# Hybrid decoder trunk: five split chunks and seven loaded ones, and the fourth block ahead of the down chunk

## What is computed

```python
for i in range(4):                     # stick-breaking, differential, forgetting, stick-breaking
    x = x + 0.5 * swiglu(rms_norm(x, norm_g[i, 0]), gate[i, 0], up[i, 0], down[i, 0])
    q, k, v = split(rms_norm(x, norm_g[i, 1]) @ w_qkv[i])
    x = x + attention_i(q, k, v) @ w_o[i]
    x = x + 0.5 * swiglu(rms_norm(x, norm_g[i, 2]), gate[i, 1], up[i, 1], down[i, 1])
return rms_norm(x, final_g)
# x: 256 tokens x 1024, d_ff 2816, 8 heads of 128, float32; swiglu(h) = (silu(h@gate) * (h@up)) @ down
```

## Time and profile before

| | |
|---|---|
| time, 3 runs | median 1882.12 us (1881.24 to 1883.84) |
| profiled execution, its own time | 1877.97 us |
| its span, first to last instruction | 1876.2 us |
| busy in the span | PE 1853.3, weight loads 1566.1, DVE 1562.6, ACT 1166.9, POOL 60.3 us |
| granted TensorE clock | 0.999 of full speed |
| DMA | 417 MB, mean 222 GB/s |

### The profile page before, as it was taken

How to read it: one execution, slowest core, us unless ns; L and a number is a source line. 1 busy time by engine, 2 the same in 40 slices (tenths; PEclk the granted TensorE clock), 3 DMA queues, 4 the chain that set the end, 5 groups by cost and what they waited for, 6 DMA issues and landing times.

```text
span 1876.2 us, 22732 instructions
## 1 busy us (share of the span) xinstructions
PE 1853.3 (99%) x9268; PEld 1566.1 (83%) x9268; DVE 1562.6 (83%) x1295; ACT 1166.9 (62%) x1220; POOL 60.3 (3%) x75
## 2 busy tenths in 40 slices
PE   9999999999999999999999999999999999999998
PEld 7788898888878899788888888987888888998886
DVE  7979568989888969998988995788898898569896
ACT  6666456666656645666665674465667567556665
POOL 1000000000000000100000000010000000001000
PEclk9999999999999999999999999999999999999999
DMA  8775445776677543577667763467775766437762
GB/s 300 261 290 226 180 157 180 226 289 264 200 249 272 235 151 134 183 254 286 266 187 272 255 247 121 149 227 245 270 278 190 274 221 246 157 108 252 277 238 79
DMA packets 59272, 417.28 MB, mean 222 GB/s; under 512 B 7192, under 2 KB 7456, under 8 KB 8992
## 3 DMA queue, kind: packets, MB, share of 16 engines
q1 hardware_dynamic: 53968, 380.09, 51.8%
q0 software_dynamic: 4608, 33.56, 9.5%
q10 hardware_dynamic: 592, 2.17, 0.3%
HBM read 414.74 MB, written 1.06 MB: 222 GB/s over the span
## 4 chain that ended last, share of the span: by engine, by line
PE 80%; DVE 12%; DMA 4%; ACT 2%; issue 2%; POOL 0%; SPq 0%; POOLq 0%; DVEq 0%; ACTq 0%
PE work L1493 16%; PE work L1495 16%; PE work L1494 16%; PE acc L1493 9%; PE acc L1495 9%; PE acc L1494 9%; DVE w_lo L919 6%; DMA extra<-stream_dram 3%; DMA raw<-stream_dram 1%; PE work L1687 1%; DVE raw L935 1%; PE acc L1537 1%; DVE raw L931 1%; PE work L1865 1%; PE work L1729 0%
## 5 line engine op out<-in xcount | busy, mean ns | idle before, releaser
L919 DVE TENSOR_TENSOR w_lo<-raw,w_hi 128x2048 fp32r<-128x2048 f32 x359 | 810.3, 2284 | 14.2 <-ACT w_hi L535 14.0
L535 ACT ACTIVATE w_hi<-raw 128x2048 fp32r<-128x2048 f32 x359 | 677.1, 1910 | 128.7 <-DVE raw L935 76.2
L1493 PE MATMUL work<-w_hi,xg 128*128 128x512 f32 x880 | 346.6, 394 | 1.1 <-DVE w_lo L919 1.1
L1495 PE MATMUL work<-w_hi,xg 128*128 128x512 f32 x880 | 343.5, 390 | 0.0
L1494 PE MATMUL work<-w_lo,xg 128*128 128x512 f32 x880 | 343.0, 390 | 0.0
L1493 PE MATMUL acc<-w_hi,m_hi 128*128 128x512 f32 x824 | 328.3, 398 | 6.3 <-DVE w_lo L919 6.1
L1495 PE MATMUL acc<-w_hi,m_lo 128*128 128x512 f32 x824 | 321.8, 391 | 0.0
L1494 PE MATMUL acc<-w_lo,m_hi 128*128 128x512 f32 x824 | 321.2, 390 | 0.0
L1495 PE MATMUL work<-w_hi,wide_r 128*128 128x512 f32 x512 | 199.8, 390 | 0.0
L1493 PEld LDWEIGHTS work<-w_hi,xg 128*128 128x128 f32 x880 | 165.4, 188 | 34.9 <-DVE w_lo L919 1.7
L1495 PEld LDWEIGHTS work<-w_hi,xg 128*128 128x128 f32 x880 | 165.3, 188 | 34.8
(11 more groups left out here) (211 smaller groups left out, 2324.8 us busy)
## 6 DMA issues: line engine op xcount, KB each, us to landing
raw<-stream_dram SPq DMA_DIRECT2D x295, 1024.0 KB, 7.3
extra<-stream_dram SPq DMA_DIRECT2D x64, 1024.0 KB, 4.9
extra<-stream_dram POOLq DMA_DIRECT2D x32, 1024.0 KB, 8.0
x<-x_dram SPq DMA_DIRECT2D x2, 512.0 KB, 8.2
raw<-stream_dram ACTq DMA_DIRECT2D x2, 512.0 KB, 8.0
scratch<-cum_rows ACTq DMA_DIRECT2D x1, 1024.0 KB, 6.5
cst<-consts_dram SPq DMA_DIRECT2D x1, 832.0 KB, 6.4
out_dram<-x SPq DMA_DIRECT2D x3, 256.0 KB, 2.5
```

What stands on the lines that cost most here:

```text
L535: nc.scalar.activation(w_hi[:, c % RING, :], raw_at(place), ACT.Copy).then_inc(hi_ready, 1)
L919: nc.vector.tensor_tensor(w_lo[:, c % RING, :], raw_at(place), w_hi[:, c % RING, :].bitcast(F32), ALU.subtract).then_inc(lo_ready, 1)
L1493: nc.tensor.matmul(dst, a_hi, b_hi, start=start, stop=False, skip_group_check=skip)
L1495: return nc.tensor.matmul(dst, a_lo, b_hi, start=False, stop=stop, skip_group_check=skip)
```

## The change

The ring of split chunks has five places, not six, and there are seven buffers of loaded chunks, not five. In the first pair of a chain b22 stands ahead of the down chunk, on PE and in the ring. With it, ACT and DVE treat the block c12 ahead of c21 in such a pair, and DVE makes the form t3' after `gate_21`. The load of b22' is listed ahead of b21' (before: after the down chunk). Where unit 1 is followed by the chain, DVE makes t3 and the third low part of the token sums before `hidden_lo(0)` in all FFNs but the first. In the differential attention a chunk is split earlier, on ACT before `mix`, on DVE before `apart_mean` and the early updates. At the end of the run the squares and the scaled output are taken from the accumulators, without the halved copy.

```diff
-RAW = 5
+RAW = 7
-RING = 6
+RING = 5
@@ pair_order, first pair of a chain
-    return [..., ("t3", s), ("down", s - 1), ("t4", s), ("b22", s)]
+    return [..., ("t3", s), ("b22", s), ("down", s - 1), ("t4", s)]
@@ plan
+            if what == "t4" and j in SEVEN[:-1] and not chained(following(j)):
+                loads.append(("b22", layer, n % 3, following(j), EXTRA, ("lo", c0 + order.index(("b22", j)) + 1)))
+            if what == "b21" and chained(j):
+                loads.append(("b22", layer, n % 3, j, EXTRA, ("lo", c0 + order.index(("b22", j - 2)) + 1)))
             for load in ("b12",) if what == "t1" else () if what in (*FORMS, "b22") else (what,):
...
-            if what == "down" and chained(j + 2):
-                loads.append(("b22", layer, n % 3, j + 2, EXTRA, ...))
...
-            if what == "t4" and j in SEVEN[:-1] and not chained(following(j)):
-                loads.append(("b22", layer, n % 3, following(j), EXTRA, ...))
@@ ACT, pair_step, first pair
                     silu_22()
+                    split_to(q + 9)
+                    silu_12()
                     split_to(q + 10)
                     silu_21()
                     split_to(q + 11)
-                    silu_12()
@@ ACT, last norm
-                        update(n, i)
-                        square_sum(n, i)
+                        last_square_sum(i)
@@ DVE, plain_step(1), not in the first FFN
+                        token_sums_lo((0, 1, 2))
                     form("t3", q)
+                        hidden_lo(0)
@@ DVE, first_of_chain
                         if s == SEVEN[0]:
                             hidden_lo(s - 1)
-                        split_to(q + 5)
-                        if s == SEVEN[0]:
                             token_sums_lo((3,))
                         split_to(q + 6)
                         gate_11()
                         sum_22()
                         split_to(q + 7)
+                        sum_12()
                         split_to(q + 8)
                         gate_22()
-                        split_to(q + 9)
+                        gate_12()
+                        split_to(q + 10)
+                        gate_21()
                         form("t3", q + 8)
-                        gate_21()
-                        sum_12()
-                        split_to(q + 10)
                         form("t2", q + 8)
-                        gate_12()
                         hidden_lo(s)
                         split_to(q + 11)
@@ DVE, end of the differential attention
                         apart_split(b)
+                        split_to(c0 + ATT_CHUNKS + 1)
+                        apart_mean()
                         for i in range(BANKS - 1):
                             early_update(i)
-                        apart_mean()
-                        split_to(c0 + ATT_CHUNKS + 1)
@@ PE, pair_step, first pair
                     quarter(chain, sum_of(S3), at["t3"], False, False)
+                    if s == SEVEN[0]:
+                        pe.wait_ge(token_lo_ready, BANKS * (f + 1))
+                    quarter(3, sum_of(S4), at["b22"], False, True)
                     unit_down(s - 1).then_inc(down_used, 1)
                     pe.wait_ge(pair_sums_ready, 2 * p + sum_count("c22"))
                     quarter(chain, block_of(1, 1), at["t4"], False, True)
-                    if s == SEVEN[0]:
-                        pe.wait_ge(token_lo_ready, BANKS * (f + 1))
-                    quarter(3, sum_of(S4), at["b22"], False, True)
```

More of the change, by code:

```diff
@@ L76, in pair_order @@
                 ("down", s - 1), ("t4", s)]
-    return [("b11", s), ("t1", s), ("t2", s), ("b21", s), ("t3", s), ("down", s - 1), ("t4", s), ("b22", s)]
+    return [("b11", s), ("t1", s), ("t2", s), ("b21", s), ("t3", s), ("b22", s), ("down", s - 1), ("t4", s)]
 def following(s):
@@ L85, in part_count, with block_count @@
     return [part for part, unit in pair_order(s) if unit == s].index(what) + 1
-def block_count(s, which):
-    return (("c11", "c22", "c12", "c21") if chained(s) else ("c11", "c22", "c21", "c12")).index(which) + 1
+def block_count(which):
+    return ("c11", "c22", "c12", "c21").index(which) + 1
 def sum_count(which):
@@ L184, in plan @@
                 loads.append((load, layer + 1, 0, SEVEN[0], place, ("lo", c0 + order.index((last, SEVEN[-1])) + 1)))
-            if what == "down" and chained(j + 2):
-                loads.append(("b22", layer, n % 3, j + 2, EXTRA, ("lo", c0 + order.index(("b22", j)) + 1)))
             if what == "down" and j + 1 in SEVEN[:-1]:
                 loads.append(("b11", layer, n % 3, following(j + 1), SUMS, ("lo", c0 + order.index(("t1", j + 1)) + 1)))
-            if what == "t4" and j in SEVEN[:-1] and not chained(following(j)):
-                loads.append(("b22", layer, n % 3, following(j), EXTRA, ("lo", c0 + order.index(("b22", j)) + 1)))
     return uses, loads
@@ L795, in attention @@
                         weights(b)
+                    if j == PAIRS and kind == DIFF:
+                        split_to(c0 + ATT_CHUNKS + 1)
                     if j < PAIRS:
@@ L830, in square_sum, with last_square_sum @@
                 nc.scalar.activation(squares[i % 2], x_part(bank), ACT.Square, scale=D ** -0.5,
+                                     accum_out=sums[:, bank // TB, bank % TB:bank % TB + 1]).then_inc(squares_ready, 1)
+            def last_square_sum(i):
+                n, bank = NORMS - 1, banks_of(NORMS - 1)[i]
+                act.wait_ge(acc_ready, BANKS * (n - 1) + i + 1)
+                act.wait_ge(squares_ready, BANKS * n + i - 1)
+                nc.scalar.activation(squares[i % 2], acc[:, bank, :], ACT.Square, scale=D ** -0.5,
                                      accum_out=sums[:, bank // TB, bank % TB:bank % TB + 1]).then_inc(squares_ready, 1)
@@ L1038, in plain_step @@
                     q = c0 + FFN_ORDER.index(("b11", s + 1))
-                    if s == 1:
+                    if s == 1 and n:
+                        token_sums_lo((0, 1, 2))
+                    elif s == 1:
                         token_sums_lo((0, 1))
@@ L1455, in next_input @@
                     final_output(0, 0)
+                    final_mean(1)
                     final_gained()
-                    final_mean(1)
                     final_output(0, 1)
@@ L1463, in final_mean @@
                 dve.wait_ge(squares_ready, BANKS * (NORMS - 1) + 2 * tb + 2)
-                nc.vector.scalar_tensor_tensor(out=mean[:, tb:tb + 1], in0=sums[:, 0, tb:tb + 1], scalar=EPS,
+                nc.vector.scalar_tensor_tensor(out=mean[:, tb:tb + 1], in0=sums[:, 0, tb:tb + 1], scalar=4 * EPS,
                                                in1=sums[:, 1, tb:tb + 1], op0=ALU.add,
@@ L1471, in final_output @@
                 dve.wait_ge(final_loaded, 16)
-                part = x_part(TB * half + tb)
-                nc.vector.scalar_tensor_tensor(out=part, in0=part, scalar=r_col[:, tb:tb + 1],
+                bank = TB * half + tb
+                nc.vector.scalar_tensor_tensor(out=x_part(bank), in0=acc[:, bank, :], scalar=r_col[:, tb:tb + 1],
                                                in1=final_gain[:, half * HALF_D:(half + 1) * HALF_D],
@@ L1682, in pair_hidden @@
                     for block in ("c12", "c22") if second else ("c11", "c21"):
-                        pe.wait_ge(pair_h_ready, 4 * p + block_count(first, block))
+                        pe.wait_ge(pair_h_ready, 4 * p + block_count(block))
                     for t in range(2):
```

21 lines of the change are left out of this document (11 added, 10 removed).

## The result

The changed kernel took 1867.06 us in the median of 5 runs (1866.86 to 1867.81), the kernel before 1881.24 us in 5 runs (1874.98 to 1883.84). The ratio is 0.9926 with a 95% interval of 0.9911 to 0.9942: faster by 14.2 us. The profiled execution of the changed kernel took 1867.57 us, 10.4 us less than that of before (1877.97). Note also the spread: 8.9 us before, 0.95 us after. In the changed kernel the lines have other numbers: the matmuls L1493 to L1495 are L1504 to L1506, the split L919 is L929, t3's form L931 is L941, `gate_21` L1084 is L1098.

A forecast was written before the change was run, and what follows sets the result against it. PE, busy 99% of the span, bounds the kernel, so only its waits can be won. Chains 6.8, first FFN 1.7 and end 0.6 sum to 9.1 us off 1882.1: 1873.0 us, range 1868 to 1881.

The forecast's parts named there:

- The chain's source: At unit 2 of later FFNs: DVE idles 3.33 us for b22' before t3', and later work queues behind it.
- The chains, 6.8 us: Chains after the first FFN: 5.0 us of listed PE waits times 1.36, all won; bounds 5.0 and 7.5.
- The load "which SP could issue only at 525.02": Load of b22', third FFN: issued once b22 was split; issue moves from 17.25 to 10.9 after b11, taking 8.0 us.
- "The median of the runs is 4.15 us above that execution, so 1882.1 - 9.1": Whole run: the 9.1 us gain is taken off the median of 1882.1 us, giving 1873.0.
- Differential attention, "nothing gained or lost": DVE's earlier split before `apart_mean` ends at 761.25, before PE's sums at 761.6, so no gain or loss.
- First FFN, 1.7 us: First FFN: gain of 1.7 us out of 5.3 us of listed PE waits; bounds 0 and 5.3.
- Tail 0.6: End of the run: ACT's 0.60 us halving leaves the path after the last matmul, gaining 0.6 us.
- Seams 0: Ends of FFNs under the ring of five: no cost taken; bounds 0 and 0.6 us for each of seven seams.
- Rival A: Ring short of room: ACT's copies wait for places, chains lose 0.85 us each; 1879 to 1883 us, chance 0.09.
- Rival B: POOL's accumulating DMA lands late, beyond 12.5 us, delaying t1' and DVE; at 14.5 us 1891, slower, chance 0.11.
- Rivals C and D: C: chains still lose 0.1 to 0.2 us, 1874.6 to 1877.9, chance 0.12. D: load still waits, 1881.5, chance 0.04.
- The sign of being wrong: PE's waits behind `w_lo` staying above 4 us would show the forecast to be wrong.

The follow-up runs named there:

- Experiment 4: The kernel before, unaltered, measured again with two more profiled executions: 1880.56 us in 12 runs, the profiled ones 1883.98 and 1876.51 us.
- experiment 2: The kernel before with only the two sizes changed, ring of five and seven buffers of loaded chunks: 1870.53 us, 0.9947 of before.
- experiment 3: The kernel before with the ring of five and six buffers of loaded chunks: 1872.61 us, 0.9961 of before.
- experiment 5: The changed kernel with the load of b22' listed at its old place in the queue, after the down chunk: 1866.77 us, 0.9930 of before.
- experiment 6: The kernel before with only `gate_21` moved ahead of forming t3': 1878.05 us in 12 runs, 0.9985 of before.
- experiment 1: The changed kernel with the old sizes, ring of six and five buffers of loaded chunks: 1867.41 us, 0.9929 of before.
- experiment 9: The kernel before with the ring of five, seven buffers and the changed kernel's order at the differential attention's end: 1869.27 us, 0.9943 of before.
- Experiments 7: The changed kernel with DVE's split put back behind `apart_mean` in the differential attention: 1870.52 us, 0.9945 of before; the other execution took 1870.60 us.
- experiment 8: The changed kernel with `apart_mean` last, behind the split and the three early updates: 1868.46 us, 0.9937 of before.

## Why the prediction was right and wrong

The mechanism was right, and the time 1867.06 lies 0.9 us below the range (1868 to 1881), 5.9 below the forecast of 1873.0. Two steps failed: the median's distance of 4.15 us, kept as if the change left it alone, and the differential attention, put at nothing. The profiled execution came out at 1867.57 against 1868.9: 1.6 us more than forecast in the attention, 0.3 in the chains and 0.4 at the start, 0.4 us less in the first FFN, 0.1 in the tail and 0.5 in the rest. A part of the closeness is thus errors that cancel. Point by point:

- **The chain's source**, DVE's wait for b22' with `gate_21`, a split, a form and the down chunk queued behind it: shown. Experiment 4 shows it as one relation over 21 chains, experiments 2, 3, 5 and 6 move its terms one by one.
- **The chains, 6.8 us**: 7.1 measured in the profiled execution. (The factor 1.36 is 1.39 by the numbers beside it, 2.33 by 1.68, which gives 6.9.) The walk through DVE's queue had the down chunk's split end at 33.5; it ends at 33.49. `gate_21` waits 0.43 us for ACT there, t3' starts at 26.1 (walked 26.06).
- **The load "which SP could issue only at 525.02"** was only half of the cause. I read the earlier trace rows as a load issued too late, and took its 8.0 us as given. Experiment 2 shows that the issue may stay where it is if little else moves beside the transfer. The change makes both repairs, and in the execution read each alone clears the seven chains: the early issue with 4.7 us or more between the landing and t3' (experiments 1 and 5), the sizes narrowly (t3' at up to 22.99 against 23.02, and one chain late in experiment 9).
- **"The median of the runs is 4.15 us above that execution, so 1882.1 - 9.1"**: this step failed, and it is the largest error. It took the distance of the median as something that the change leaves in place. Yet the delay itself is what scatters: 7.1 us in the execution that I read, 12.0 in one at 1883.98, 4.8 in one at 1876.51. An execution at the median has more delay to lose. The forecast for the execution, 1868.9, carried over to the median without the 4.15 us, would have been 1.8 us too high.
- **Differential attention, "nothing gained or lost"**: failed, 1.6 us. I weighed the split's move on DVE alone and did not price what ran beside it on POOL. The row of a pow beside a split was in the trace, 2.53 us, and so was PE's wait of 1.49 us for x behind it. In the kernel before DVE's split (both inputs in SBUF) starts at 761.71 and ends at 763.99, the pow starts at 761.87 and ends at 764.40, 0.41 after it: blocked, then done. In the changed kernel the updates beside it read one input from PSUM. Experiments 7 to 9 turn it on and off. The split and the updates differ in length too (2048 and 512 columns), and the runs do not part the two; but the second pow of the changed kernel lies inside the second of the three updates (757.82 to 758.50) and ends at 758.45, before it, so that update did not block it. The Trainium skill, SBUF — State Buffer, Who interferes with whom, says that `tensor_tensor` with both inputs in SBUF contends with GpSimd's reads. The same page, SBUF: two separate sides, says that whichever starts first holds the shared ports for the whole instruction while the other is blocked. The rows agree, with 2.53 us against 0.55.
- **First FFN, 1.7 us**: 1.3 in this stage between the two executions read. Over seven executions with the new order the stage takes 181.1 to 182.2 us, mean 181.6, over the three of the kernel before 183.5 to 184.4, mean 184.1: the gain is nearer to 2.5, and the term was 0.8 too small. (With the old order the two runs with the seven buffers take 182.5 and 182.7 us, so the sizes seem to carry a part of it.) PE still comes late to the down chunk of unit 2 (78.10) and to unit 6 (101.44).
- **Tail 0.6**: 0.5, and 0.5 with the tail alone undone.
- **Seams 0**: the FFNs 2 to 8 are 0.5 us longer in all outside their chains, within the bounds. This is all that the ring of five costs.
- **Rival A** showed its sign, ACT's L535 waiting for PE, 40 times and 51 us in all, and not its price. The copies wait, but the cover before their splits holds: no chain is late, and experiment 1 shows that a sixth place takes the waits away and gives nothing that the times show.
- **Rival B** named a real effect in the wrong size: the accumulating transfers grew from 8.0 to 10.5 us in the median, with the sizes alone to 12.4. In the changed kernel they took 12.0 us at most, inside the 12.5 us of cover that I gave them, and ACT waited for two of them, in the first FFN. With the sizes alone they took up to 14.4 us and in experiment 5 up to 14.6, ACT waited 11.6 and 7.9 us for them, and still no chain outside the first FFN was late: the cover was larger than my walk had it. Rivals C and D did not occur.
- **The sign of being wrong**, waits behind `w_lo` above 4 us, came up by a hair: 3.4 + 0.7 = 4.1 us, all in the first FFN, where 3.6 of the 5.3 us were forecast to stay.

What is left open: the transfer's 4.8 to 8.1 us goes with how much else moves while it is under way (2.8 MB against 1.5 in experiment 2), but how much each load ahead and behind counts, and why it varies between executions, was not tried. The buffers were tried alone only with the ring of five, and the ring of five not with five buffers. Nor was it tried what ends the stretch at the lower clock.

## What to carry to other kernels

Look at the spread of the times before you use their median: where a kernel scatters by 9 us and the wait that you remove ends with a transfer, the wait is likely what scatters, and the gain is to be taken from an execution at the median, not added to one at the edge. A load that arrives late can be cured by an earlier issue or by less traffic beside it, and a change that does both should be tried with each alone before one is credited. And when an instruction is moved, look at what ran beside it on the engine that shares its port, as well as at its own queue.

## What was not expected of the hardware

- A `pow` of one column on GpSimd takes 0.55 us, and 2.53 us beside a VectorE `tensor_tensor` of 128x2048 float32 that reads two SBUF operands (2.28 us), in all eight executions with the split beside it. Beside updates of 128x512 with one operand in PSUM, or with VectorE idle, it takes 0.55, in all six others. The pow behind it starts 2.50 us after it in the first case and 0.51 in the second.
- The same load of 1 MB landed 4.8 to 8.1 us after its issue, from one execution of one kernel to the next. The delays behind it sum to 4.8 us in one execution and 12.0 in another, 7 us of a difference of 7.5 in their times.
- A wait of TensorE of 1.49 us made the differential attention 1.6 us longer. One of 2.02 us made it 3.6 longer, since 1.5 us more went in a stretch at the lower clock.
